# Splitting the experts' weights a whole raw tile at a time in a two-block transformer kernel

## The reference

```python
y = jnp.zeros_like(xt)
for e in range(N_EXPERTS):
    h = jax.nn.silu(xt @ w_gate[e]) * (xt @ w_up[e])
    y = y + gate[:, e:e + 1] * (h @ w_down[e])
```

## Time and profile before

| | |
|---|---|
| Median of 3 runs | 1902.42 us (1900.78 to 1905.46) |
| Profiled execution, its own time | 1904.23 us |
| Its span, first to last instruction | 1902.4 us |
| Busy in the span | PE 83%, weight loads (PEld) 69%, DVE 69%, ACT 60%, POOL 2% |
| Mean granted clock of PE | 0.916 |
| Moved by DMA | 422.75 MB, mean 222 GB/s |

### The profile page before, as it was taken

How to read it: one execution, slowest core, us unless ns; L and a number is a source line. 1 busy time by engine, 2 the same in 40 slices (tenths; PEclk the granted TensorE clock), 3 DMA queues, 4 the chain that set the end, 5 groups by cost and what they waited for, 6 DMA issues and landing times.

```text
span 1902.4 us, 20940 instructions
## 1 busy us (share of the span) xinstructions
PE 1581.5 (83%) x7971; PEld 1312.5 (69%) x7971; DVE 1315.8 (69%) x1784; ACT 1132.2 (60%) x1335; POOL 32.9 (2%) x67
## 2 busy tenths in 40 slices
PE   4989867999986879985899998498997778999875
PEld 3769755777775769864777776387786556877754
DVE  3657355898897476436898888547555568988963
ACT  3534425888885443432888888256453258888862
POOL 4000000000000100000000000000000000000000
PEclk7989888899998889987999999699987889999988
DMA  8345323999997434621899999243432339999960
GB/s 274 110 151 201 113 89 135 328 345 345 367 348 277 156 133 136 216 70 67 297 346 355 350 341 365 91 153 114 133 122 97 125 107 351 348 356 358 365 234 22
DMA packets 174628, 422.75 MB, mean 222 GB/s; under 512 B 7036, under 2 KB 7200, under 8 KB 174512
## 3 DMA queue, kind: packets, MB, share of 16 engines
q1 hardware_dynamic: 170336, 407.92, 61.0%
q0 software_dynamic: 4176, 13.30, 2.2%
HBM read 420.15 MB, written 1.05 MB: 221 GB/s over the span
## 4 chain that ended last, share of the span: by engine, by line
PE 47%; DVE 24%; DMA 12%; ACT 10%; issue 6%; DVEq 0%; SPq 0%; ACTq 0%
DVE w_low L1447 13%; PE ps L568 10%; PE ps L569 9%; PE ps L570 9%; DMA raw<-in_w_gate 9%; ACT w_high L1149 6%; PE ps L762 5%; PE ps L788 3%; PE ps L749 2%; DMA raw<-in_w_up 2%; ACT work L1221 2%; PE ps L799 1%; DVE out_low L1679 1%; PE ps L645 1%; DMA raw<-in_w_in 1%
## 5 line engine op out<-in xcount | busy, mean ns | idle before, releaser
L1447 DVE TENSOR_TENSOR w_low<-raw,w_high 128x1024 fp32r<-128x1024 f32 x774 | 908.7, 1220 | 335.7 <-ACT w_high L1149 334.1
L1149 ACT ACTIVATE w_high<-raw 128x1024 fp32r<-128x1024 f32 x774 | 784.5, 1053 | 455.5 <-PE ps L570 352.1
L568 PE MATMUL ps<-w_high,act_high 128*128 128x512 f32 x464 | 191.2, 412 | 41.4 <-DVE act_low L1467 25.8
L569 PE MATMUL ps<-w_low,act_high 128*128 128x512 f32 x464 | 187.7, 405 | 0.0
L570 PE MATMUL ps<-w_high,act_low 128*128 128x512 f32 x464 | 186.8, 403 | 0.0
L788 PE MATMUL ps<-w_high,hT 128*128 128x512 f32 x384 | 161.1, 420 | 0.0
L788 PE MATMUL ps<-w_low,hT 128*128 128x512 f32 x384 | 160.5, 418 | 0.0
L762 PE MATMUL ps<-w_high,x_odd 128*128 128x512 f32 x384 | 152.2, 396 | 0.0
L762 PE MATMUL ps<-w_low,x_odd 128*128 128x512 f32 x384 | 150.2, 391 | 0.0
L568 PEld LDWEIGHTS ps<-w_high,act_high 128*128 128x128 f32 x464 | 91.7, 198 | 66.3 <-issue 47.3
L570 PEld LDWEIGHTS ps<-w_high,act_low 128*128 128x128 f32 x464 | 91.4, 197 | 20.3
(11 more groups left out here) (350 smaller groups left out, 2565.2 us busy)
## 6 DMA issues: line engine op xcount, KB each, us to landing
raw<-in_w_gate SPq DMA_DIRECT2D x96, 1024.0 KB, 7.0
raw<-in_w_up SPq DMA_DIRECT2D x96, 1024.0 KB, 7.2
raw<-in_w_down SPq DMA_DIRECT2D x96, 1024.0 KB, 7.3
raw<-in_w_in SPq DMA_DIRECT2D x44, 1024.0 KB, 5.6
raw<-in_w_out SPq DMA_DIRECT2D x12, 1024.0 KB, 4.9
raw<-in_wk_x SPq DMA_DIRECT2D x8, 1024.0 KB, 5.4
raw<-in_wv_x SPq DMA_DIRECT2D x8, 1024.0 KB, 4.9
raw<-in_wq_x SPq DMA_DIRECT2D x8, 1024.0 KB, 7.7
```

The costliest lines, as they stand in the source:

```text
L568: pe.matmul(out, lh, rh, start=first, stop=False)
L569: pe.matmul(out, lh, rl, start=False, stop=False)
L1149: A(split_unit(n)[0], raw_unit(n), ACT.Copy).then_inc(high_ready, 1)
L1447: V.tensor_tensor(split_unit(n)[1], raw_unit(n), split_unit(n)[0].bitcast(F32), ALU.subtract).then_inc(low_ready, 1)
```

## The change

In the experts' loop (`experts_own`) ACT and DVE make the high and the low parts for a whole raw tile, 2,048 columns, in one operation where they made two of 1,024. Each operation counts its semaphore up by 2. ACT waits until PE has used both units that stood in the place of the two; DVE waits for the high parts of both. The order of the splits among the other work, SP's transfers, PE's program and every split outside `experts_own` (and in `experts_all`) stay as they are.

```diff
+        def pair_of_units(tile, u):
+            return tile[:, u % SPLIT:u % SPLIT + 2, :].rearrange("p u n -> p (u n)")
...
+            def split_pairs(count):
+
+                nonlocal n
+                for _ in range(count // 2):
+                    if n < N_UNITS:
+                        c = n // 2
+                        act.wait_ge(loaded[c % RAW], 16 * (c // RAW + 1))
+                        wait_unit_used(act, n + 1 - SPLIT)
+                        A(pair_of_units(w_high, n), raw[:, c % RAW, :], ACT.Copy).then_inc(high_ready, 2)
+                    n += 2
...
                     if e:
                         silu(e - 1)
-                        split(2 if e < NE else 0)
+                        split_pairs(2 if e < NE else 0)
                         hidden(e - 1)
-                        split(2 if e < NE else 0)
+                        split_pairs(2 if e < NE else 0)
                     if e < NE - QUAD:
                         packed(e // QUAD + 1, e % QUAD, YS)
                     if e < NE:
-                        split(4)
+                        split_pairs(4)
                         gate_up(e)
-                        split(2)
+                        split_pairs(2)
                         places_turned(e)
-                        split(2)
+                        split_pairs(2)
                     if e:
                         output(e - 1)
-                split(4)
+                split_pairs(4)
...
+            def split_pairs(count):
+
+                nonlocal n
+                for _ in range(count // 2):
+                    if n < N_UNITS:
+                        dve.wait_ge(high_ready, n + 2)
+                        V.tensor_tensor(pair_of_units(w_low, n), raw[:, n // 2 % RAW, :], pair_of_units(w_high, n).bitcast(F32),
+                                        ALU.subtract).then_inc(low_ready, 2)
+                    n += 2
...
                     if e:
                         product(e - 1)
-                        split(2 if e < NE else 0)
+                        split_pairs(2 if e < NE else 0)
                         hidden(e - 1)
-                        split(2 if e < NE else 0)
+                        split_pairs(2 if e < NE else 0)
                     if e < NE:
-                        split(4)
+                        split_pairs(4)
                         slot_gates(e)
-                        split(4)
+                        split_pairs(4)
                     if e:
                         output(e - 1)
-                split(4)
+                split_pairs(4)
```

## The result

| | before | after |
|---|---|---|
| Median, 7 runs each | 1902.42 us (1893.26 to 1906.63) | 1925.5 us (1914.29 to 1934.85) |
| Ratio after to before | | 1.0119, 95% interval 1.008 to 1.0158 |
| Profiled execution, span | 1902.4 us | 1912.6 us |

Predicted were 1908 us and at most 1924; the kernel became 23 us slower, 1.5 us beyond the range. The profiled execution of the changed kernel is its fastest of seven. Its three stages, each from the end of the routing to the start of the norm (or of the copy that follows the third), together take 953.4 us against 933.7 before, +19.7. Everything outside them takes 959.2 us against 968.7, though nothing was changed there; the profiles of the experiments have 963 to 974. So I read the stages and leave the rest aside.

What follows compares the result with a forecast made beforehand. Weight transfers were taken as the bound, PE close behind. Openings +4, drains +1.5 and steady part 0 gave +5.5 us on the median of 1902.4: 1908 us, range 1894 to 1924 (the forecast's own 1903 to 1914).

Steps and rivals of the forecast that it cites:

- (b): Readiness at second down and next first gate tile: releases about 1 us later, covered by transfer queue: 0.
- (g): Steady part of the stages: a quarter of the -13.5 us gain (-3.5) plus half the +7.5 us copy delay (+3.5): 0.
- (c): ACT's copy of gate and up, queued behind next first gate tile's split: 0.5 us later in 15 experts, +7.5 us.
- (a): Fewer, longer operations on ACT and DVE: -0.3 us per expert on the transfer loop, -13.5 us over 45 experts.
- rival B: Slower: three-tile ring too coarse, ACT's split before the copy comes late; 1935 us, or 1921 with half paced; chance 0.25.
- rival A: Faster: DVE and ACT are the hidden bound, all -13.5 us of shorter operations counts: 1894 us; chance 0.15.
- (e): Opening of each stage: first copy of gate and up 1.4 us later; +1.3 us taken per stage, +4 us.
- (f): Drain of each stage: DVE idles 0.6 us for the first high tile; +0.5 us per stage, +1.5 us.
- (d): PE's own wait for the first down tile's low part: half a us of reserve left, taken as 0.

Runs made afterwards that it cites:

- open_single: Changed kernel, but 1,024-column splits in each stage's first expert ahead of its copy of gate and up: 1916.85 us, ratio 1.0072 to the kernel before.
- c_dve_only: Kernel before, with whole tiles on DVE alone at the second down and next first gate tile, experts 1 to 15: 1913.78 us, ratio 1.0043.
- c_wait_only: Kernel before, single operations; ACT only waits for both used units at second down and next first gate tile, experts 1 to 15: 1912.56 us, ratio 1.0035.
- open_only: Kernel before, with whole tiles only in the four splits of each stage's first expert ahead of the copy: 1911.03 us, ratio 1.0034.
- c_only: Kernel before, with whole tiles on both engines at the second down and next first gate tile, experts 1 to 15: 1921.86 us, ratio 1.0096.
- copy_first_singles: Kernel before, single units throughout, with ACT's copies of gate and up and of the spread one tile earlier: 1881.99 us, ratio 0.9891.
- act_pairs: Changed kernel, with DVE's low parts in two operations of 1,024 columns again, whole tiles on ACT only: 1918.33 us, ratio 1.0102 to the kernel before.

## Why the prediction was wrong

**The premise** was "the weight transfers come first and PE is close behind". The step that failed is reading the DMA share of 0.98 as transfers that could go no faster. The share hardly tells: 349 GB/s at 0.99 and 368 at 1.01, with the splits of one tile moved on ACT. With the transfers as the bound I let small delays die out, and so (b) stood at nothing and (g) added up to nothing. In fact an expert's time came from the loop through ACT's copy, PE, the spread, DVE and back, with the transfers as one leg of it. This reading is an inference from the runs with the copies moved; the loop itself was not measured leg by leg.

**(g), the steady part**: taken 0, measured +0.72% (13.7 us) with `open_single`. The two halves of the sum were: (c) "+7.5 us if nothing absorbs it", of which I took half; (a) -13.5, of which I took a quarter. In place of the sum the runs show, at D1 and G0, 0.35% (6 or 7 us) for the coarser wait, near the 7.5 of (c), and 0.43% (8 us) for the late handover, which (b) had at 0; of (a) no gain is seen in any run.

**(b), readiness**: "Cost taken: 0" for D1 and the next G0, because their transfers have 2 us of queue. The queue was there, as forecast; the landing time hardly moved (median 7.3 to 7.2 us). The cover was the wrong one: `c_dve_only` puts the late low part at +0.43% (8 us), with a median landing time of 7.1 us. That it costs through DVE's order of work and not through the transfer is my reading of this.

**(c), the copy**: the mechanism of rival B was right in part. Its place was right (ACT ahead of the copy), and so was its sign of recognition: answering to the earlier trace rows, ACT's waits for PE's up product rose and those for gate tiles fell.

```profile
  PE ps L765: 10.9, 14
...
  DMA raw<-in_w_gate: 5.1, 9
```

But B's coarser wait alone is 0.35% of the 1.19 (`c_wait_only`), and in the changed kernel PE waits less for the copy than before (63.8 against 74.7 us). B was priced at 1921 with half of the copies paced, where the kernel took 1925; that the two are so near is partly luck, since the handover and the longer openings are in the second and not in the first. Its chance was set at 0.25, for "13 waits for gate tiles". That count was misread: the earlier trace rows count both gate tiles, and by ACT's timeline only 8 of the 13 stand ahead of the copy, at G0; the other five are G1's. So 7 of the first stage's 15 copies were not led by a gate tile, where (c) had taken one in three. The Trainium skill's rule ("Perfetto Trace Analysis", section Optimizing Scalar/DVE Operations), that smaller pieces may finish sooner where an unsaturated engine causes gaps on others, is what the runs bear out: DVE and ACT were not saturated, had 34 us less to do together, and the time rose; but 0.35% come with the pieces as small as before (`c_wait_only`), from the wait alone. The same section's rule for saturated engines never came into play (rival A).

**(e), the openings**: mechanism right, size off. 4 us were taken with 5.7 as the bound, and 6.5 measured (`open_only`). The first copy came 2.2, 1.7 and 2.4 us later, not 1.4. The forecast left out the granted clock, though the list of what would prove it wrong had named it: PE stood 3.47 us and ran at the lower level of its clock behind it (0.50 from 314 to 324 us). And it took two units for 1.87 us, which take 2.13 even at the upper level.

**(f), the drain**: the idle 0.59 us came; the +1.5 us did not, since nearly all of the 2.07 us of issue ahead of the norm went away in the first two stages.

**(a) and the rest**: 1.90 and 2.29 us held, and so did (d) nearly: PE waits only 2.5 us for low parts of weights between 340 and 588 us, where it waited for none.

One sum is off without weight for the rest: the forecast's own range, by the bounds that it names, ends at 1902.4 + 5.7 + 2.6 + 2 = 1912.7 us, not at 1914.

## What to carry to other kernels

Ahead of merging operations on an engine that isn't full, look for the small result that another engine waits for and that is queued behind them in program order; move it ahead of them first. Here moving the two small copies ahead of one tile gave 1.1%, and brought what the merge costs at that place from 17 us to little or nothing; merging at all places cost 33 us even so. A DMA share near 1 doesn't prove that transfers are the bound: it takes a run in which something else gets faster.

## What the runs showed of the hardware

- The DMA share moves little where the rate moves much: 337 GB/s at 0.97 (`c_only`, 340 to 588 us), 349 at 0.99 (before, 930 to 1160 us), 368 at 1.01 (`copy_first_singles`, the same).
- After a stop of PE of 3.47 us its granted clock fell: 16 transposes took 3.51 us instead of 1.89. The stop of 1.48 us in the kernel before had left it at the upper level. In the first stage matmuls were slower from 1.5 us after PE had started again, in the second, after the same stop, only from some 5.5 us after it (16 transposes in 2.18 us).
- The 2.07 us of issue between DVE's last split and the first norm operation shrank to 0.14 when the last splits became two operations instead of four, with a wait of 0.59 us for ACT ahead of them. The size of DVE's operations is not the reason: in `act_pairs` DVE has the same four as before, with a wait of 0.52 us ahead of them, and 0.11 us are left. In every kernel where DVE runs these four without a wait it is about 2 us. What goes on in the gap no run shows.
